# Three in-projection blocks of layer 0 multiplied as three rounded fp32r products each instead of one fp32 product

## What is computed

```python
def _layer(x, ...):
    proj = einsum('btd,de->bte', x, w_in)              # the in-projection: 1024 -> 23 tiles of 128 columns
    hq, hf, hi, hg, rq, rk, rv, rg, su = split(proj)   # hi, rv: values; rq, rk: retention; hg, rg: gates
    o_hg = gated linear recurrence(silu(hq), k(hf), hi, log f(hf))     # HGRN2 heads
    o_rt = retention(rotary(rq), rotary(rk), rv)
    y5   = gelu/GLU of an S5 scan of su
    x = layer_norm(ALPHA * x + concat(o_hg, o_rt, y5) @ w_out)
    return layer_norm(ALPHA * x + square(relu(x @ w_up)) @ w_down)
```

## Time and profile before

| what | us |
|---|---|
| median of 3 executions | 741.53 |
| lowest, highest | 739.55, 748.14 |
| the profiled execution | 747.85 |
| its span, first to last instruction | 746.1 |
| TensorE busy | 716.9 |
| VectorE busy | 536.8 |
| ScalarE busy | 411.5 |

### The profile page before, as it was taken

One profiled execution on the slowest core, in us unless ns is written; L12 is line 12 of the kernel. 1 busy time (PEld: TensorE's weight loads), 2 busy tenths in 40 slices (PEclk: granted clock), 3 DMA queues, 4 the chain that ended last, 5 costly groups with the idle time before them and its releaser, 6 DMA issues. The chain is left out here.

```text
span 746.1 us, 17512 instructions
## 1 busy us (share of the span) xinstructions
PE 716.9 (96%) x7224; PEld 661.0 (89%) x7224; DVE 536.8 (72%) x969; ACT 411.5 (55%) x771; POOL 40.6 (5%) x54
## 2 busy tenths in 40 slices
PE   8999899999999999999989999999999999999994
PEld 7788768869999999999979887877999999999993
DVE  7978864378787988874775987556878776555474
ACT  5533043456687566773558423365568755677342
POOL 1100102100000000000040002020000000000001
PEclk9999898999999999999999999999999999999998
DMA  7831124436465555565524312342636555655531
GB/s 257 306 115 59 60 86 159 168 97 193 136 194 171 181 189 186 180 184 156 178 78 141 96 51 86 132 152 62 221 116 200 185 179 178 188 174 190 177 113 58
DMA packets 30718, 112.50 MB, mean 151 GB/s; under 512 B 3536, under 2 KB 3744, under 8 KB 30256
## 3 DMA queue, kind: packets, MB, share of 16 engines
q1 hardware_dynamic: 28080, 100.78, 42.7%
q0 software_dynamic: 1984, 9.54, 3.5%
q10 hardware_dynamic: 576, 1.08, 0.4%
HBM read 107.20 MB, written 4.18 MB: 149 GB/s over the span
## 5 line engine op out<-in xcount | busy, mean ns | idle before, releaser
L1629 DVE TENSOR_TENSOR w_low<-w_raw,w_high 128x1024 fp32r<-128x1024 f32 x161 | 197.0, 1224 | 113.0 <-ACT w_high L1146 111.1
L1146 ACT ACTIVATE w_high<-w_raw 128x1024 fp32r<-128x1024 f32 x161 | 170.4, 1058 | 150.0 <-PE stream L1086 135.5
L1084 PE MATMUL stream<-a_high,w_high 128*128 128x264 f32 x520 | 155.0, 298 | 3.1 <-DVE a_low L2239 3.0
L1085 PE MATMUL stream<-a_low,w_high 128*128 128x264 f32 x520 | 149.1, 287 | 0.0
L1086 PE MATMUL stream<-a_high,w_low 128*128 128x264 f32 x520 | 148.9, 286 | 0.0
L1084 PE MATMUL stream<-h_high,w_high 128*128 128x264 f32 x512 | 146.3, 286 | 0.0
L1086 PE MATMUL stream<-h_high,w_low 128*128 128x264 f32 x512 | 145.1, 283 | 0.0
L1085 PE MATMUL stream<-h_low,w_high 128*128 128x264 f32 x512 | 145.0, 283 | 0.0
L1084 PEld LDWEIGHTS stream<-a_high,w_high 128*128 128x128 f32 x520 | 99.5, 191 | 8.1 <-issue 5.7
L1085 PEld LDWEIGHTS stream<-a_low,w_high 128*128 128x128 f32 x520 | 99.7, 192 | 0.4
L1086 PEld LDWEIGHTS stream<-a_high,w_low 128*128 128x128 f32 x520 | 99.3, 191 | 0.0
(11 more groups left out here) (394 smaller groups left out, 995.8 us busy)
## 6 DMA issues: line engine op xcount, KB each, us to landing
w_raw<-in_weights SPq DMA_DIRECT2D x190, 512.0 KB, 3.6
mats<-in_matrices POOLq DMA_DIRECT2D x2, 1024.0 KB, 7.6
S_hg<-in_state_hg POOLq DMA_DIRECT2D x2, 768.0 KB, 5.9
out_hg_s<-S_hg POOLq DMA_DIRECT2D x2, 768.0 KB, 3.7
consts<-in_constants POOLq DMA_DIRECT2D x1, 1499.5 KB, 6.5
X<-in_xT ACTq DMA_DIRECT2D x4, 264.0 KB, 5.1
out_y<-X SPq DMA_DIRECT2D x4, 264.0 KB, 2.1
S_rt<-in_state_rt POOLq DMA_DIRECT2D x2, 512.0 KB, 6.7
```

What stands on the lines that cost most here:

```text
L1084: pe.matmul(bnk[:, 0:width], wh, xh, start=(first and kk == 0), stop=False)
L1085: pe.matmul(bnk[:, 0:width], wh, xl, start=False, stop=False)
L1146: act.activation(w_high[:, SPLIT_SLOT[n], :], w_raw[:, RAW_SLOT[n], :], ACT.Copy).then_inc(high_ready, 1)
L1629: put(tt(w_low[:, SPLIT_SLOT[n], :], w_raw[:, RAW_SLOT[n], :], w_high[:, SPLIT_SLOT[n], :].bitcast(F32), ALU.subtract), low_ready)
```

## The change

One number in the table of unsplit blocks:

```diff
-UNSPLIT = (tuple(_c for _c in range(OUT0 + 2) if not 18 <= _c <= 22), (*range(12, 19), OUT0, OUT0 + 1))
+UNSPLIT = (tuple(_c for _c in range(OUT0 + 2) if not 15 <= _c <= 22), (*range(12, 19), OUT0, OUT0 + 1))
```

## The result

| | before | after |
|---|---|---|
| median, us | 740.74 (4 executions, 739.55 to 748.14) | 752.28 (4 executions, 750.98 to 754.19) |
| ratio to before | | 1.0135, 95% interval 1.0097 to 1.0173 |
| profiled execution | 747.85, span 746.1 | 752.15, span 750.4 |
| TensorE busy | 716.9 | 716.5 |

The changed kernel is slower, by 1.35%.

What follows compares the result with a forecast made beforehand. TensorE sets the end, with VectorE level in steps 13 to 18. Walking both engines gave 1.9 us late, 749.8 on the profiled execution; on the median 743.4 to 746.6, with most of the stall and clock terms about 747.0, range 741 to 753.

Steps and rivals of the forecast that it cites:

- the 5 us for executions without the stall: Start of block 18: without step 14's 2.83 us stall and slow block 15, the change costs about 5 us.
- TensorE's gain: Blocks 15 to 17: split products save 1.0 + 0.66 + 0.66 = 2.3 us if nothing waits.
- No room on VectorE: Steps 14 to 16: four `w_low`, 4.9 us, land ahead of L1863 on an engine without gaps.
- The wait before L791 of step 16: After block 16: TensorE waits 1.1 us for the bank that L1863 frees, spending its whole gain.
- L886 in step 16: Retention scores ahead of block 17: L886 begins at 105.4 in place of 104.32.
- The new wait of step 18: Block 20's `w_high` waits for block 17, VectorE waits a microsecond behind it; block 18 starts 1.9 us late.
- The clock: New waits may drop TensorE's clock for block 17: 5.44 in place of 3.10 us, everything behind 2.3 later.
- The gap between profile and median: Profiled execution 6.3 us above the median; step 14's stall and slow block 15 make 5.3, probably missing from faster executions.
- All of it is hidden: Rival: waits for L1863 and block 20's `w_high` are hidden, only 2.3 us of products goes: 739.2; chance 0.12.
- Slower beyond the measurable: Rival: clock drops in step 16's first new wait, block 17 runs at 1.2 GHz: 748.9 to 753; chance 0.17.
- Block 18 turns fast: Rival: block 18 takes 3.10 in place of 5.44 us, giving back the 1.9: 741; chance 0.09.
- The stall, if it is code loading: Rival: step 14's stall is instruction fetching; others come or go, 2.8 us each: 744 to 750; chance 0.07.

Runs made afterwards that it cites:

- e2: Kernel before with blocks 15 to 17 as fp32r products of one stand-in block, no weights split for them: 743.00 us, ratio 0.9989.
- e3: Changed kernel with its splits kept, but TensorE multiplying the rounded weights of blocks 15 to 17 as fp32: 750.20 us, ratio 1.0086.
- e11: Kernel before with one idle product at the start replaced by 25 tiny ones, shifting TensorE's code: 746.12 us, ratio 1.0055.
- e5: Changed kernel with the GELU argument ahead of the two `w_low` of step 16 on VectorE: 749.54 us, ratio 1.0090.
- e9: Changed kernel with block 20 alone moved back to being split one step ahead of use: 749.35 us, ratio 1.0103.
- e7: Kernel before with only block 17 newly split and block 20 moved one step forward: 745.36 us, ratio 1.0022.
- e4: Changed kernel with blocks 18 to 20 moved back to being split one step ahead of use: 746.39 us, ratio 1.0035.
- e6: Changed kernel with blocks 18 to 20 moved back and the GELU argument ahead of step 16's `w_low`: 746.19 us, ratio 1.0040.
- e10: Changed kernel with blocks 18 to 20 moved back and `w_low` of blocks 15 to 17 on GpSimd: 747.26 us, ratio 1.0084.
- e8: Kernel before with 48 more small products at the start of TensorE's program, shifting its code: 767.10 us, ratio 1.0319.
- e12: Kernel before with block 18 left unsplit too, the opposite edit: 744.18 us, ratio 1.0017.
- e1: Kernel before, unedited, run again for a second profile: 741.13 us, ratio 0.9956.

## Why the prediction was right, and where it was too small

I gave 747.0, a range of 741 to 753, and 0.34 for slower by over 1%, 0.63 for within it. It came to 752.28, inside the range, in the direction named, at its upper end and on the side that I had held less likely: 11.5 us in place of 5.5. The places of the waits were right. The sum was less so, and that it came as near as it did is partly luck: its largest term, the 5 us for executions without the stall, rested on a reading that the runs refute, and stood in for a clock term that was too small. Step by step:

- *TensorE's gain.* Block 15 took 5.17 us (5.2 said), block 16 about 3.1 before its wait. The gain is real, arrives only in part even when it costs nothing (e2), and in the changed kernel not at all. (The profile records 16 more instructions for a split block, where the prediction counts 32; the time of the step doesn't rest on it.)
- *No room on VectorE.* Right, shown by the missing gaps and by e3 and e11. (There is one gap above half a microsecond in the stretch that I called free of them: 0.70 us before L1894 at 72.70, in which VectorE waits for its own L1910.) Four `w_low` were to cost 4.9 us; they cost 5.7, because two of them ran beside GpSimd (3.25 us in place of 2.46). Taking out the 0.6 us by which this profile is later from block 14 on, L1863 ended at 101.5 where I had said 100.8.
- *The wait before L791 of step 16.* Said 1.1, measured 1.03; e5 shows it was for L1863.
- *L886 in step 16.* Said 105.4; 106.87, or 106.3 less the 0.6.
- *The new wait of step 18.* Its mechanism was right: the rows after show ScalarE held by block 17 and VectorE behind it, and e9 takes both away. Its size was not: I had VectorE waiting one microsecond, and it waited 3.80, because block 17 was slow. With block 17 at full clock and the same move, e7 has no such wait, and the `w_low` itself makes TensorE wait.
- *The clock,* the term that was mis-sized. The walk had block 17 at full clock; the slow one was a term of 2.3 us of which the 747.0 took an unnamed part, and a rival with 0.17. It took 5.15 us in place of 3.10, and since `w_high` of block 20 waits for it, its 2 us went straight through the wait of step 18. Block 18 starts 5.7 us later against block 14 than in the first profile, where I had 1.9. Of the difference of 3.8, 0.9 are there at the first L886 (mostly the L1863 above), 0.7 are L886 and L889 at the lower clock, and 2.1 block 17. The stall of step 14, 0.8 longer than in the first profile, adds nothing to it, since TensorE then waited for L1863 all the same. In all eight profiles with more waiting in step 16 than before (0.8 us in e3, 1.5 and more in after, e4, e5, e6, e9, e10 and e11) block 17 is slow, between 4.3 and 5.6 us. In the six with 0.35 to 0.67 there (both of the kernel before, e2, e7, e8, e12) it is at full clock. It was the likely case.
- *The gap between profile and median.* Wrong reading. I had the stall of step 14 missing from the faster executions. It is in all profiles without shifted code, 2.4 to 3.6 us, also in e1 at 740.65. Nor would its absence have put block 18 some 4 us earlier in the kernel before: in e11 it is as good as gone, and block 18 starts where it did in e1. The first profile was slow by its slow stretches: two of 6.8 and one of 3.4 us before block 25, where e1 has one of 3.4. So what I took for the lower bound (1.9 on the median) was no bound at all; the sum should have been made from block 14 to 18 with the clock of both executions, and against e1 it is 31.3 to 38.9, and 34.3 to 43.6 at the end of block 18: 9.3 of the 11.5 us. Of the rest 1.6 lies ahead of block 14, where executions differ anyway.
- *The rivals.* "All of it is hidden" is out. "Slower beyond the measurable" had this case, 748.9 to 753: the clock falls in the new waits, though by the rows only at the last of the three. "Block 18 turns fast" did not happen in the changed kernel, though it does in e4, e6, e9, e10 and e11, where block 17 is slow and no wait follows it. The stall, if it is code loading, changes with shifted code (e8, e11), but the three blocks stand behind it.

What stays open: how much of the changed kernel's loss is waiting and how much clock. The two feed each other, and I have no run with the waits and without the slow stretches. That the waits bring the slow stretch is a pattern in eight profiles against six, one execution each, and not a cause shown by itself. Open too is what makes the stall of step 14.

## What to carry to other kernels

An engine at 72% of the span can have no room at all in the steps where work is added: count its gaps there, not its share. A change in when something is prepared can cost more than the added preparation, if the earlier place puts a wait for the bound engine in front of work that this engine is waiting for; e4, with the move undone, got back 6.3 of the 7.6 us at block 18 (not all of it by that, since its slow stretches are shorter too), and e9, with one of the three blocks moved back, 2.7. And where the trace shows a slow stretch of TensorE's clock behind small products and waits, new waits in such a place should be costed with the slow clock as the likely case.

## What the runs showed of the hardware

- A subtraction of 128 x 1024 on GpSimd takes 2.35 us and stretches VectorE's operation beside it by up to 2.26 us (e10). Two `w_low` on VectorE that take 2.35 us alone (e5) took 3.25 beside GpSimd's selection (after).
- TensorE can stand still for 2.4 to 3.6 us where it runs through a dense burst of small products, with a piece of code loaded inside the stretch. With 24 more fp32 products ahead of it in the program 0.33 us were left at the same place (e11), with 48 more there were two stalls, at two other places (e8).
- 96 records of an fp32 product with 16 columns and a full 128 x 128 stationary operand took 20.5 us, 213 ns each (e8, granted clock 1.00).
